# Attention by head pairs beside the in-projection of a hybrid decoder layer, and its weights' low halves on GpSimd

## The reference

```python
proj = x_ext @ w_in                       # 1024 -> 3*512 attention + 3*512 + 64 + 64 + 160 recurrent columns
q, k, v = cur[..., :512], cur[..., 512:1024], cur[..., 1024:1536]
s = q @ k.T * HEAD_DIM ** -0.5 - slope * dist ; p = softmax over the windows ; att = p @ v
rw = rw_cur + (rw_prev - rw_cur) * mu_shift          # token shift, then r, k, v, w_low, a_low, g_low
decay = exp(-exp(-softplus(-(w0 + tanh(w_low) @ w_lora_up)) - 0.5)); a = sigmoid(a0 + a_low @ a_lora_up)
kk = k * k_k / norm(k * k_k) ; k = k * (1 + (a - 1) * k_a)
S = S * decay + (S @ -kk) (kk * a)^T + v k^T ; y = S @ r       # over time
h = concat(att, y) @ w_out ; layer norm ; gated ConvFFN ; layer norm
```

## Time and profile before

| | |
|---|---|
| median of 3 runs | 973.67 us (972.17 to 975.32) |
| the profiled execution's own time | 975.93 us |
| its span, first to last instruction | 974.1 us |
| granted TensorE clock, mean | 0.961 of full speed |
| in-projection, first product to last bank emptied | 9.64 to 283.7 us |
| VectorE, ScalarE, GpSimd busy | 516.7, 333.2, 259.2 us |

### The profile page before, as it was taken

How to read it: one execution, slowest core, us unless ns; L and a number is a source line. 1 busy time by engine, 2 the same in 40 slices (tenths; PEclk the granted TensorE clock), 3 DMA queues, 4 the chain that set the end, 5 groups by cost and what they waited for, 6 DMA issues and landing times.

```text
span 974.1 us, 22370 instructions
## 1 busy us (share of the span) xinstructions
PE 891.2 (91%) x9660; PEld 820.4 (84%) x9660; DVE 516.7 (53%) x758; ACT 333.2 (34%) x551; POOL 259.2 (27%) x111
## 2 busy tenths in 40 slices
PE   5988989998989688798999879999999999999995
PEld 5867978787777677677998779999999999999994
DVE  4247674545656757762464446776666665000026
ACT  4464433434331202123232644433333333211124
POOL 0000000000014360801252524543444344343410
PEclk9999999999999879999999879999999999999997
DMA  7201302124126332433012203233223322323302
GB/s 255 69 23 65 98 23 86 45 69 151 33 72 157 94 88 79 121 112 133 24 49 75 65 24 108 91 107 106 89 87 88 94 100 79 100 80 94 102 2 89
DMA packets 31299, 83.42 MB, mean 86 GB/s; under 512 B 5128, under 2 KB 8392, under 8 KB 30688
## 3 DMA queue, kind: packets, MB, share of 16 engines
q1 hardware_dynamic: 30048, 79.82, 26.6%
q10 hardware_dynamic: 1152, 2.16, 0.6%
HBM read 75.87 MB, written 5.91 MB: 84 GB/s over the span
## 4 chain that ended last, share of the span: by engine, by line
PE 77%; DVE 14%; ACT 4%; issue 3%; DMA 1%; POOL 1%; ACTq 0%; DVEq 0%; POOLq 0%
PE banks L1733 76%; DVE rw L1161 2%; DVE xx L1161 1%; DVE ms L1161 1%; DVE w_lo L1161 1%; DVE pm L1161 1%; DMA att<-in_x 1%; ACT x_hi L1069 1%; ACT z L1072 1%; DVE carry L1161 1%; PE banks L1777 1%; DVE rw L1164 1%; DVE z L1161 1%; DVE z L1164 1%; DVE sw L1164 1%
## 5 line engine op out<-in xcount | busy, mean ns | idle before, releaser
L1733 PE MATMUL banks<-x_hi,w_hi 128*128 128x264 f32 (+1 forms) x784 | 215.5, 308 | 16.3 <-DVE x_lo L1161 13.6
L1733 PE MATMUL banks<-x_hi,w_lo 128*128 128x264 f32 (+1 forms) x784 | 201.3, 290 | 0.0
L1733 PE MATMUL banks<-x_lo,w_hi 128*128 128x264 f32 (+1 forms) x784 | 201.2, 290 | 0.0
L1733 PEld LDWEIGHTS banks<-x_hi,w_hi 128*128 128x128 f32 x784 | 141.6, 195 | 41.5 <-issue 26.5
L1733 PEld LDWEIGHTS banks<-x_lo,w_hi 128*128 128x128 f32 x784 | 142.4, 196 | 0.1
L648 POOL TENSOR_TENSOR w_lo<-w_raw,w_hi 128x1024 fp32r<-128x1024 f32 (+1 forms) x40 | 95.6, 2389 | 176.0 <-ACT w_hi L761 175.8
L1733 PEld LDWEIGHTS banks<-x_hi,w_lo 128*128 128x128 f32 x784 | 142.0, 195 | 0.0
L648 POOL TENSOR_TENSOR wx_lo<-w_raw,wx_hi 128x1024 fp32r<-128x1024 f32 (+1 forms) x36 | 86.1, 2392 | 100.7 <-ACT wx_hi L761 100.2
L656 POOL MEMSET kv<- 32x4608 f32 x1 | 3.9, 3938 | 282.5 <-PE banks L1733 282.5
L1164 DVE SCALAR_TENSOR_TENSOR z<-z,banks 128x260 f32<-128x260 f32 (+1 forms) x24 | 12.4, 516 | 122.5 <-PE banks L1733 115.3
L1733 PE MATMUL banks<-x_hi,wx_hi 128*128 128x260 f32 x352 | 73.6, 283 | 0.0
(11 more groups left out here) (256 smaller groups left out, 1934.2 us busy)
## 6 DMA issues: line engine op xcount, KB each, us to landing
w_raw<-in_w SPq DMA_DIRECT2D x87, 512.0 KB, 3.5
w_raw<-in_w SPq DMA_DIRECT2D x16, 448.0 KB, 3.3
kv<-in_ck SPq DMA_DIRECT2D x16, 192.0 KB, 3.6
kv<-in_cv SPq DMA_DIRECT2D x16, 192.0 KB, 3.1
att<-in_x ACTq DMA_DIRECT2D x8, 264.0 KB, 7.4
att_out<-att SPq DMA_DIRECT2D x1, 2112.0 KB, 9.2
z<-in_xc SPq DMA_DIRECT2D x1, 2080.0 KB, 7.6
y_out<-z SPq DMA_DIRECT2D x8, 260.0 KB, 2.2
```

The source lines that it names most:

```text
L1733: return pe.matmul(out, l, r, start=start, stop=stop)
```

## The change

- Attention is done in 16 ticks of two units, one tick a slot, in slots 10 to 25 (S_TICK, TICKS). Unit numbers become u = 2 k + p, with tick k = 4 c + q and p the head of pair c. The two scores stand together, on array rows 0 to 63 and 64 to 127, into banks 6 and 7; the values' products alternate between the two heads' output partitions; transposes go to banks 4 and 3. The softmax rows have four buffers in place of two.
- SLOTS is reordered: the recurrence's keys first, its values near the end. The recurrence's preparation moves to slots 2 to 9; low_rank does both kinds in one insertion, alternating array rows; key_sums moves to bank 5 and key_spread alternates between banks 6, 7 and 3, 4; transforms stand in slots 10, 14, 18 and 22, behind the softmax work.
- In VectorE's stream the order in a slot is now shift, last pair's low half, preparation, softmax of both units, division of both, transform. In ScalarE's: last bank, next high half, copies of the transposed probabilities, first bank, exponentials.
- The low halves of the in-projection's weights are made by GpSimd, at the front of its stream, instead of VectorE.
- The bias tables are loaded in pairs ahead of the weights of slots 16, 20 and 24.
- The scratch tile tmp now lies in pt.

```diff
-SLOTS = [("r", 0), ("a", 0), ("a", 4), ("a", 8), ("r", J_KS), ("r", J_KS + 1), ("r", J_KS + 2), ("r", J_KS + 3),
-         ("a", 1), ("a", 5), ("a", 9), ("r", J_RS), ("r", J_VS), ("a", 2), ("a", 6), ("a", 10),
-         ("r", J_RS + 1), ("r", J_VS + 1), ("a", 3), ("a", 7), ("a", 11), ("r", J_RS + 2), ("r", J_VS + 2),
-         ("r", J_RS + 3), ("r", J_VS + 3), ("r", 1), ("r", 2)]
+SLOTS = [("r", 0), ("r", J_KS), ("r", J_KS + 1), ("r", J_KS + 2), ("r", J_KS + 3), ("a", 0), ("a", 4), ("a", 8),
+         ("r", J_RS), ("a", 1), ("a", 5), ("a", 9), ("r", J_RS + 1), ("a", 2), ("a", 6), ("a", 10), ("r", J_RS + 2),
+         ("a", 3), ("a", 7), ("a", 11), ("r", J_RS + 3), ("r", J_VS), ("r", J_VS + 1), ("r", J_VS + 2), ("r", J_VS + 3),
+         ("r", 1), ("r", 2)]
...
+TICKS = UNITS // 2
+S_TICK = 10
+S_SHAPE = [S_TICK + TB * c for c in range(CC)]
+S_VTOK = [10, 12, 16, 20]
...
-    tmp = sb(pa, "tmp", [P, XC])
...
-    sw = sb(pa, "sw", [P, 2, T])
+    sw = sb(pa, "sw", [P, 4, T])
     pt = sb(pa, "pt", [P, 2, T])
+    tmp = pt[:, :, :].rearrange("p a t -> p (a t)")[:, 0:XC]
...
             if h >= 2:
-                sp.wait_ge(a_biased, TB * (h - 1))
+                sp.wait_ge(a_biased, H * (h // 2))
...
-        late = {10: 2, 11: 3, 16: 4, 18: 5, 21: 6, 23: 7}
         for s in range(2, N_IN):
+            if s in (16, 20, 24):
+                bias(s // 2 - 6)
+                bias(s // 2 - 5)
             weights(s)
-            if s in late:
-                bias(late[s])
-            if s == 9:
-                sp.wait_ge(lora_ps, 2 * CC)
+            if s == 6:
+                sp.wait_ge(lora_ps, CC)
                 sp.dma_start(low_up[:], a["bsel"]).then_inc(bsel_landed, 16)
             if s == 25:
                 sp.wait_ge(in_copied, 2 * v_slots[-1] + 2)
...
+        for s in range(N_IN):
+            pool.wait_ge(w_hi_ready, s + 1)
+            pool.tensor_tensor(w_lo[:, s % 2, :], w_raw[:, s % 2, :], w_hi[:, s % 2, :].bitcast(F32), ALU.subtract)\
+                .then_inc(w_lo_ready, 1)
+            own(w_lo_ready)
...
             ac.wait_ge(a_probs_t, u + 1)
-            if u >= 2:
-                ac.wait_ge(a_pv, u - 1)
-            ac.activation(pt[:, u % 2, 0:n], banks[:, 4, 0:n], ACT.Copy).then_inc(a_pt, 1)
+            if k >= 1:
+                ac.wait_ge(a_pv, k)
+            ac.activation(pt[:, u % 2, 0:n], banks[:, 4 - u % 2, 0:n], ACT.Copy).then_inc(a_pt, 1)
...
+        def low_sigmoid(c):
+            ac.wait_ge(lora_ps, c + 1)
+            for dst, bias, b in ((yy, C_W0, 6), (aa, C_A0, 3)):
+                ac.activation(dst[:, c, :].rearrange("p (a b) -> p a b", a=2), banks[:, b:b + 2, 0:XH], ACT.Sigmoid,
+                              bias=col(bias + c)).then_inc(lora_out, 1)
+                own(lora_out)
...
-            if s - 1 in v_slots:
-                v_tok_copy(v_slots.index(s - 1))
-            if s in (12, 17, 22, 24):
-                decays((12, 17, 22, 24).index(s))
-            for half in range(2):
-                if 2 <= s < 2 + CC:
-                    low_sigmoid(2 * (s - 2) + half)
-                if (s, half) in ticks:
-                    att_tick(ticks[s, half])
-                if half == 1 and 5 <= s < 5 + CC:
-                    key_square(s - 5)
-                if (s, half) == (9, 1):
-                    ac.wait_ge(kk_cl, 1)
-                    ac.activation(knorm[:, :], knorm[:, :], ACT.Sqrt).then_inc(n_root, 1)
-                    own(n_root)
-                if half == 0 and s < N_IN:
-                    evac(s, 0)
+            if s >= S_TICK + TB + 1 and (s - S_TICK - 1) % TB == 0:
+                att_mix((s - S_TICK - 1) // TB - 1)
+            if s in S_VTOK:
+                v_tok_copy(S_VTOK.index(s))
+            if s in S_SHAPE:
+                decays(S_SHAPE.index(s))
+            if s in (2, 3):
+                low_sigmoid(2 * (s - 2))
+            if s == 7:
+                ac.wait_ge(kk_cl, 1)
+                ac.activation(knorm[:, :], knorm[:, :], ACT.Sqrt).then_inc(n_root, 1)
+                own(n_root)
+            k = s - S_TICK
+            if 1 <= k <= TICKS:
+                pt_copy(2 * k - 2)
+                pt_copy(2 * k - 1)
+            if s < N_IN:
+                evac(s, 0)
+            if s in (2, 3):
+                low_sigmoid(2 * (s - 2) + 1)
+            if 2 <= s < 2 + CC:
+                key_square(s - 2)
+            if 0 <= k < TICKS:
+                att_exp(2 * k)
+                att_exp(2 * k + 1)
...
-        def w_low(s):
-            ve.wait_ge(w_hi_ready, s + 1)
-            tt(w_lo[:, s % 2, :], w_raw[:, s % 2, :], w_hi[:, s % 2, :].bitcast(F32), ALU.subtract).then_inc(w_lo_ready, 1)
-            own(w_lo_ready)
-
-        w_low(0)
...
+            if u >= 4:
+                ve.wait_ge(a_probs_t, u - 3)
+            ve.wait_ge(a_scores, k + 1)
+            stt(x, banks[:, 6 + u % 2, 0:n], HD ** -0.5, abias[:, h % 2, T - n:T], ALU.mult, ALU.add).then_inc(a_biased, 1)
             own(a_biased)
-            ve.tensor_reduce(nmax[:, u:u + 1], sw[:, u % 2, 0:n], AX, ALU.max, negate=True).then_inc(a_max, 1)
+            ve.tensor_reduce(nmax[:, u:u + 1], x, AX, ALU.max, negate=True).then_inc(a_max, 1)
...
-            tt(kk2, kk2, banks[:, 6:8, 0:XH], ALU.mult).then_inc(kk_ap, 1)
+            b = 3 if c % 2 else 6
...
-            if s + 1 < N_IN:
-                w_low(s + 1)
-            if 5 <= s < 5 + CC:
-                key_in(s - 5)
-            if s in (12, 17, 22, 24):
-                transform((12, 17, 22, 24).index(s))
...
+            if s >= S_TICK + TB + 1 and (s - S_TICK - 1) % TB == 0:
+                mix_lo((s - S_TICK - 1) // TB - 1)
+            if 2 <= s < 2 + CC:
+                key_in(s - 2)
+            if 3 <= s < 3 + CC:
+                decay_sums(s - 3)
+            if s == 7:
+                ve.wait_ge(n_sum, CC)
+                ve.tensor_scalar(knorm[:, :], banks[:, 5, 0:SUM], 1e-24, None, ALU.max).then_inc(kk_cl, 1)
+                own(kk_cl)
+                ve.wait_ge(n_root, 1)
+                link(ve.reciprocal(knorm[:, :], knorm[:, :]))
+                tt(kbig[:, :].rearrange("p (g t) -> p g t", g=4), knorm[:, :].unsqueeze(1).broadcast_to([P, 4, SUM]),
+                   par[:, C_QUAD:C_QUAD + 4].unsqueeze(2).broadcast_to([P, 4, SUM]), ALU.mult).then_inc(n_inv, 1)
+                own(n_inv)
+                ve.wait_ge(lora_out, 2 * CC)
+                ve.tensor_copy(gath[:, :, 1, :], yy[:, :, T + 1:XC:2]).then_inc(ga_done, 1)
+                own(ga_done)
+            if s in (8, 9):
+                key_norm(2 * (s - 8))
+                key_norm(2 * (s - 8) + 1)
+            k = s - S_TICK
+            if 0 <= k < TICKS:
+                for p in range(2):
+                    soft(2 * k + p)
+                for p in range(2):
+                    scale(2 * k + p)
+            if s in S_SHAPE:
+                transform(S_SHAPE.index(s))
...
-            if c >= 1:
-                pe.wait_ge(a_pt, H * c - 2)
+            if c == 0:
+                pe.wait_ge(kk_ap, CC)
+            else:
+                pe.wait_ge(a_pt, 2 * (S_VTOK[c] - S_TICK - 2) + 1)
...
+        def scores(k):
+            c, q = divmod(k, TB)
+            n = (q + 1) * P
+            if k == 0:
+                pe.wait_ge(kk_ap, CC)
+            else:
+                pe.wait_ge(a_biased, 2 * k)
+            for p in range(2):
+                ins = mm(banks[:, 6 + p, 0:n], att[half_rows(p), c, q * P:q * P + P], att[half_rows(p), CC + c, 0:n])
+            ins.then_inc(a_scores, 1)
+
+        def probs_t(k, p):
+            u = 2 * k + p
             pe.wait_ge(a_norm, u + 1)
-            pe.wait_ge(v_tok, min((u + 2) // H + 1, CC))
-            if u >= 1:
-                pe.wait_ge(a_pt, u)
-            for j in range(u % TB + 1):
-                ins = pe.transpose(banks[:, 4, j * P:(j + 1) * P], sw[:, u % 2, j * P:(j + 1) * P], ident[:, :])
+            if p == 0:
+                pe.wait_ge(v_tok, sum(v <= S_TICK + 1 + k for v in S_VTOK))
+            if k >= 1:
+                pe.wait_ge(a_pt, u - 1)
+            for j in range(k % TB + 1):
+                ins = pe.transpose(banks[:, 4 - p, j * P:(j + 1) * P], sw[:, u % 4, j * P:(j + 1) * P], ident[:, :])
             ins.then_inc(a_probs_t, 1)
 
...
+        def values(k):
+            c, q = divmod(k, TB)
+            pe.wait_ge(a_pt, 2 * k + 2)
+            if q == 0 and c >= 1:
+                pe.wait_ge(a_mix_hi, c)
+                pe.wait_ge(a_mix_lo, c)
             for j in range(q + 1):
-                ins = mm(banks[lo:lo + 64, 5, q * P:(q + 1) * P], vtok[:, j, h * HD:(h + 1) * HD],
-                         pt[:, u % 2, j * P:(j + 1) * P], j == 0, j == q)
+                for p in range(2):
+                    h = 2 * c + p
+                    ins = mm(banks[half_rows(p), 5, q * P:(q + 1) * P], vtok[:, j, h * HD:(h + 1) * HD],
+                             pt[:, p, j * P:(j + 1) * P], j == 0, j == q)
```

(93 more changed lines are left out.)

58 lines of the change are left out of this document (14 added, 44 removed).

## The result

| | before | changed |
|---|---|---|
| median | 974.35 us (4 runs, 972.17 to 975.32) | 922.01 us (4 runs, 918.04 to 924.45) |
| ratio, 95% interval | | 0.9462 (0.9423 to 0.9501) |
| profiled execution, own time (span) | 975.93 (974.1) | 918.04 (916.2) |
| last large product of the in-projection | 282.9 us | 226.7 us |
| in-projection: idle time of TensorE for sw | 17.1 us | none |

The change makes the kernel 5.4% faster, 52 us in the medians. Two executions of later runs, of 2759 us (experiment 8) and of 2088 us (the kernel before, in the rounds of experiments 9 to 11), are left out of their ratios, since all others of a kernel lie within 1.5% of each other. The profiled execution of the changed kernel happens to be the fastest of the four.

What follows compares the result with a forecast made beforehand. TensorE, busy 91% of the span, was taken as the bound: only less TensorE time or fewer waits help. Gains 34.0 + 17.1 + 8 less costs 5.0 give 54 us, from 973.67 to 920 us, range 912 to 941.

Steps and rivals of the forecast that it cites:

- likeliest case: Whole kernel: the forecast of 920 us holds, within its own range 912 to 931; chance 0.67.
- Pairs overlap fully: In-projection insertions: two heads cost what one did, saving 14.8 us for scores, 14.1 for values, 5.1 for low rank.
- The rival on overlap: In-projection pairs: row halves don't overlap, 932 us, or no halves do, 941 us; chance 0.17.
- No wait for sw, and no half clock behind it: In-projection: all 17.1 us of TensorE's idle time for softmax rows goes, and 8 us of half clock with it.
- the five stretches of its sum: In-projection: half clock after five long idle times, 1.7 us lost for each, 8.4 us, taken as 8.
- GpSimd's low halves: In-projection weights: 33 us leave VectorE, GpSimd takes 2.39 us each, but VectorE's two-operand steps can lose up to 2.4 us a slot.
- small waits in slots 3 to 10: In-projection: late sigmoids and key scaling cost 2 us, from 0 to 8.
- its own account of the tick: In-projection slot with four key blocks: softmax rows done near 6 us, exponentials near 7, of 9 us; nothing is close.
- The start: First slots: TensorE starts 1.1 us later, plus half of a possible 2.4 us stall: cost 2.3 us, bounds 1.1 and 3.5.
- The end: End of the in-projection: the attention output's last low half delays the copies that the first mask waits for, 0.7 us.
- Rivals on GpSimd: In-projection: GpSimd's subtraction is 1 us late in each slot, 947 us, chance 0.10; or GpSimd becomes the bound, 998, chance 0.04.
- the other side: In-projection: GpSimd becomes the bound, with 11 us a slot and 998 us in all; chance 0.04.

Runs made afterwards that it cites:

- experiment 8: Kernel of experiment 1 with the last pair's copy and low half ahead of the last bank and last shift: 914.7 us, ratio 0.9358.
- experiments 9 to 11: Kernel of experiment 1 again, 913.0 us; that with transforms ahead of softmax steps, 914.74 us; kernel before with transforms behind softmax units, 976.97 us.
- Experiment 2: Changed kernel with the two scores of a pair in different gaps, so that they can't overlap: 933.61 us, ratio 0.9574.
- experiment 4: Kernel before with only the low halves of the in-projection weights moved to GpSimd: 988.11 us, ratio 1.0116.
- experiment 11: Kernel before with each transform behind the slot's two softmax units instead of ahead of them: 976.97 us, ratio 0.9996.
- experiment 1: Changed kernel with all 27 low halves of the in-projection weights back on VectorE: 914.06 us, ratio 0.9356.
- experiment 10: Kernel of experiment 1 with the four transforms ahead of the slot's softmax steps: 914.74 us, ratio 0.9375.
- the repeat: Changed kernel measured once more with no edit: 923.13 us, ratio 0.9438.
- experiment 3: Changed kernel with all values' key blocks of the first head ahead of the second's, still one insertion: 926.17 us, ratio 0.9479.

## Why the prediction was right

The prediction was 920 us, range 912 to 941, likeliest case 912 to 931; measured are 922.01 and, repeated, 923.13. The mechanism of its gains is right. That the time is so near is in part luck: between the two profiled executions the terms come to 34.1 us for pairs, 17.1 for waits and 9.5 by difference for the half clock behind them (with some small waits), less 3.5 for late steps of VectorE and 1.0 for the start, and 1.7 gained behind the last bank, together 57.9. A lost race takes 4.7 off, which leaves 53 against the predicted 54, but with costs of 9.2 us where the prediction had 4.3 without the end, offset by gains 1.6 us larger and an end that gained 1.7 where it was to cost 0.7. By its steps:

- **Pairs overlap fully: 34.0 us.** Right, and to the size. Insertions of two heads measure 0.63, 0.85, 1.06 and 1.27 us start to start for scores (one head before: 0.63, 0.84, 1.05, 1.27), values 0.58 to 1.24 as before, and a low-rank pair 1.30 us as one had. Experiment 2 takes the scores' share back: 13 us in the measured time, 15 in the trace, against 14.8. The rival on overlap is out, for the 64 by 128 form too. The values' and the low-rank products' shares are read from the profile alone.
- **No wait for sw, and no half clock behind it: 17.1 + 8 us.** Right: none is left and the granted clock is 1.00 from 16 to 226 us. The chain that the prediction read ahead of the late step, shift and w_lo, is no full account of the cause. Taking w_lo away alone made it worse (experiment 4), and moving the transforms away alone moved the waits (experiment 11). In the new round VectorE carries w_lo without loss (experiment 1), and the transforms' old place on top costs 2 us, which the intervals can't tell from nothing (experiment 10). The new round as a whole does it: a score bank for each head, four softmax buffers, and results that are wanted a slot later. Which of these is needed was not separated. The prediction's reading of the idle times also missed one: 2.29 us at 186 us in the kernel before, as long as three of its five. Behind it the granted clock stays 1.00 (188.3 to 192 us), so the five stretches of its sum stand. And VectorE's input comes 2.5 us into a slot with four key blocks (scores at 109.87, bias step at 111.14 us, slot from 108.67), where the prediction wrote 2.9 and its own terms add up to 2.7; nothing hangs on it.
- **GpSimd's low halves.** VectorE's 33 us go, but they were worth nothing: experiment 1 is 0.8% faster than the changed kernel (0.9356 against 0.9438, 8 us) and has them all on VectorE. The prediction named the cost, VectorE's two-operand steps held during a subtraction, and put small waits in slots 3 to 10 at 2 us; they measure 3.5 us against experiment 1 (0.9, 1.2, 0.6 and 0.8 us in slots 8, 10, 12 and 23), two of them beyond the slots that it named. It did not ask whether the move was needed, though its own account of the tick left 2 us of VectorE's time free in each slot.
- **The start: 2.3 us, between 1.1 and 3.5.** The mechanism and both its cases are right, the term is mis-sized: 1.0 us where VectorE comes first, but 5.7 us where GpSimd does, since the prediction counted the stall of 2.4 us and not the half speed that goes on for 6 us behind it. If most executions are of the second kind, which the times suggest and don't prove, the term is nearer 5. One of its signs did not come: VectorE's first low half of x was to start near 9.9 us, and it starts at 8.12 and is held until GpSimd is done (it ends at 10.63); the first product is late all the same.
- **The end: 0.7 us.** The first mask moves from 4.9 to 6.1 us behind the last bank's copy, 1.2 us: the chunk products ran at half speed (0.43 us apart, 0.22 in the earlier trace rows) after TensorE's 3.1 us of idle time, which the prediction had taken to be covered. The next steps gave it back and 0.5 us more, by what experiment 8 shows: before, TensorE idled 2.68 us ahead of 290.59 us and the granted clock was 0.50 from 290.6 to 297; in the changed kernel it was still busy, and the clock 1.00 from 235.6 to 240.3. From the first mask to VectorE's next step on a bank it takes 8.87 us before and 7.15 after.
- **Rivals on GpSimd.** Its subtraction was never late in a slot: TensorE waited for w_lo at the start alone. But experiment 4 shows that the other side was no remote case for this part by itself: in the old round it costs 12 us by the medians, with 1.1 at the start, 4.7 by the race, and the rest in longer waits for sw and what comes behind them, since the transforms' first step is held.

The Trainium skill's rule on the shared port (SBUF — State Buffer, SBUF: two separate sides) is borne out here. During the subtraction of 101.60 us a softmax step with its scores in PSUM is not held. A step of the transform at 93.90 us, with two SBUF tensors, meets the subtraction of 93.55 us and takes 2.80 us; the next, behind it, takes 0.69. VectorE's timeline and GpSimd's in the changed kernel:

```profile
93.55 2.60 POOL L656 TENSOR_TENSOR w_lo<-w_raw,w_hi 128x1024 fp32r<-128x1024 f32 x1 [5.72 <-ACT w_hi L748]
93.90 2.80 DVE L1166 TENSOR_TENSOR aa<-aa,ksq 128x512 f32<-128x512 f32 x1
96.73 0.69 DVE L1166 TENSOR_TENSOR rw<-rw,ksq 128x512 f32<-128x512 f32 x1
...
101.60 2.41 POOL L656 TENSOR_TENSOR w_lo<-w_raw,w_hi 128x1024 fp32r<-128x1024 f32 x1 [5.46 <-ACT w_hi L748]
...
102.80 0.56 DVE L1169 SCALAR_TENSOR_TENSOR sw<-banks,abias 128x384 f32<-128x384 f32 x1 [2.20 <-PE banks L1727]
```

## What to carry to other kernels

Inserted products of half the array's rows or columns should stand in pairs, alternating halves, in one gap: the second costs nothing here, 34 us in all by the insertions' lengths, and apart the scores alone cost 13 us more. Before work is moved from VectorE to GpSimd, ask what TensorE would still wait for without the move: here nothing, and the move cost 8 us of the 60 that were to be had. The best version measured is the change with the low halves left on VectorE, ratio 0.9356 twice; where work must go to GpSimd, keep it from becoming ready just as VectorE's last urgent two-operand step does.

## What the runs showed of the hardware that was not expected

A step of VectorE with one SBUF tensor can be held as well: the 128x4 scaling of a parameter took 2.27 us during GpSimd's second subtraction and 0.17 us outside one (in the repeat, at 17.89 us). In VectorE's timeline of the changed kernel:

```profile
15.72 2.27 DVE L1176 TENSOR_SCALAR onemka<-par 128x4 f32<-128x4 f32 x1
```

Which engine comes first hangs on 0.2 us: GpSimd, ready at 14.87 us, goes ahead of VectorE's last low half, and ready at 15.04 it goes behind it. Behind a stall of 2.3 us at the start, products stand 0.22 us apart instead of 0.12 for some 3 to 6 us, whether they had come to 0.12 before it (18.7 to 21.9 us in experiment 2, granted clock 0.51; 18.0 to 24.0 in experiment 4, 0.50) or not (to 23.6 us in the repeat). An idle time of 2.29 us at 186 us in the kernel before left the granted clock at 1.00. And products on different column halves overlap over a distance of about two products when they are not alternated (experiment 3).
